# Seven products in another order, a convolution moved to VectorE, and embedding products placed around the last group of a two-block transformer kernel

## What is computed

```python
def conv_glu(h, w_gate, w_up, conv_w, conv_b, w_down):   # block 1, width 2816
    a = h @ w_gate
    u = h @ w_up
    c = conv_b
    for j in range(3):
        c = c + ap[:, j:j + S] * conv_w[j]        # ap: a padded by one token on each side
    return (gelu(c) * u) @ w_down
...
x = x + conv_glu(rmsnorm(x, norm_ffn_g), ...)
gate = sigmoid(rmsnorm(x, norm_ple_g) @ w_ple_gate)
x = x + (p @ w_ple) * gate                         # p: 256 wide, "the embedding"
...
f = square(relu(rms_norm(h, norm2_g) @ w_ff1))     # block 2, width 4096
h = h + f @ w_ff2
gate = sigmoid(rms_norm(h, norm3_g) @ w_ple_gate_2)
h = h + gate * (p_2 @ w_ple_proj_2)
```

## Time and profile before

| | |
|---|---|
| median of 3 runs (3089.62 to 3100.17) | 3090.14 us |
| the profiled execution, its time | 3095.22 us |
| its span in the profile | 3093.4 us |
| TensorE busy | 2879.4 us (93%) |
| VectorE, GpSimd, ScalarE busy | 1841.7, 1183.8, 1010.8 us |
| mean granted clock of TensorE | 0.972 of full speed |

### The profile page before, as it was taken

One profiled execution on the slowest core, in us unless ns is written; L12 is line 12 of the kernel. 1 busy time (PEld: TensorE's weight loads), 2 busy tenths in 40 slices (PEclk: granted clock), 3 DMA queues, 4 the chain that ended last, 5 costly groups with the idle time before them and its releaser, 6 DMA issues. The chain is left out here.

```text
span 3093.4 us, 36229 instructions
## 1 busy us (share of the span) xinstructions
PE 2879.4 (93%) x14210; PEld 2339.4 (76%) x14210; DVE 1841.7 (60%) x2219; ACT 1010.8 (33%) x1476; POOL 1183.8 (38%) x730
## 2 busy tenths in 40 slices
PE   8999999999689898898969999999989999999879
PEld 6888888877577677777748866678868888888767
DVE  8666577776555555555575766663855555555545
ACT  5555433232322222222233344441232222222331
POOL 3111111125555554445534411123555554555332
PEclk9999999999899999999989999999999999999989
DMA  3111001021011111111111200011211111111102
GB/s 119 31 32 30 27 28 35 28 72 38 32 47 45 45 47 45 42 45 44 48 48 66 79 22 21 21 34 35 102 34 52 51 53 55 48 55 52 62 28 81
DMA packets 60767, 145.12 MB, mean 47 GB/s; under 512 B 7616, under 2 KB 8384, under 8 KB 60352
## 3 DMA queue, kind: packets, MB, share of 16 engines
q1 hardware_dynamic: 56288, 128.83, 13.0%
q10 hardware_dynamic: 4320, 14.09, 1.2%
HBM read 132.05 MB, written 8.49 MB: 45 GB/s over the span
## 5 line engine op out<-in xcount | busy, mean ns | idle before, releaser
L892 PE MATMUL ps<-a_hi,w_hi 128*128 128x512 f32 x1184 | 493.2, 417 | 11.6 <-POOL w_lo L766 10.6
L894 PE MATMUL ps<-a_hi,w_lo 128*128 128x512 f32 x1184 | 467.9, 395 | 0.0
L893 PE MATMUL ps<-a_lo,w_hi 128*128 128x512 f32 x1184 | 467.0, 394 | 0.0
L1949 DVE TENSOR_TENSOR x<-ps,x 128x512 f32<-128x512 f32 x432 | 296.8, 690 | 284.4 <-PE ps L1030 283.5
L813 POOL TENSOR_TENSOR w_lo<-w_raw,w_hi 128x512 fp32r<-128x512 f32 x206 | 281.5, 1371 | 395.0 <-ACT w_hi L2279 394.2
L761 POOL TENSOR_TENSOR w_hi<-w_raw,der 128x1024 fp32r<-128x1024 f32 (+1 forms) x61 | 112.7, 1847 | 735.7 <-PE ps L894 568.1
L766 POOL TENSOR_TENSOR w_lo<-w_raw,w_hi 128x1024 fp32r<-128x1024 f32 (+1 forms) x78 | 204.0, 2615 | 286.3 <-ACT w_hi L2279 217.5
L2279 ACT ACTIVATE w_hi<-w_raw 128x512 fp32r<-128x512 f32 (+1 forms) x223 | 145.6, 661 | 453.7 <-PE ps L1030 275.7
L892 PEld LDWEIGHTS ps<-a_hi,w_hi 128*128 128x128 f32 x1184 | 226.3, 191 | 51.6 <-issue 12.4
L894 PEld LDWEIGHTS ps<-a_hi,w_lo 128*128 128x128 f32 x1184 | 225.4, 190 | 49.8
L893 PEld LDWEIGHTS ps<-a_lo,w_hi 128*128 128x128 f32 x1184 | 226.7, 191 | 37.9 <-issue 0.2
(11 more groups left out here) (385 smaller groups left out, 6322.7 us busy)
## 6 DMA issues: line engine op xcount, KB each, us to landing
w_raw<-in_w_mix SPq DMA_DIRECT2D x54, 512.0 KB, 3.5
w_raw<-in_w_f SPq DMA_DIRECT2D x96, 256.0 KB, 2.6
w_raw<-in_w_gu SPq DMA_DIRECT2D x88, 256.0 KB, 2.6
w_raw<-in_w_ple SPq DMA_DIRECT2D x20, 512.0 KB, 3.5
chunk<-in_w_f SPq DMA_DIRECT2D x32, 256.0 KB, 3.1
chunk<-in_w_dn SPq DMA_DIRECT2D x22, 256.0 KB, 3.1
w_raw<-in_w_dn SPq DMA_DIRECT2D x22, 256.0 KB, 3.0
x<-in_x SPq DMA_DIRECT2D x8, 512.0 KB, 7.8
```

The costliest lines, as they stand in the source:

```text
L892: mm(ps[:, bank, :], wh, hi[:, k, cols], start=(k == 0), stop=False)
L893: mm(ps[:, bank, :], wh, lo[:, k, cols], start=False, stop=False)
L894: last = mm(ps[:, bank, :], wl, hi[:, k, cols], start=False, stop=(k == nk - 1))
L1949: tt(x[:, u, c], ps[:, 5 + (2 * KT * (ff.group0 + g) + n) % 3, :], x[:, u, c], ALU.add).then_inc(x_add, 1)
```

## The change

The same products are computed with the same number of matmuls. What moves:

1. **Order of the seven products**: A22, S1, S3, A11, S2, A12, S4, and the down product of the last group goes ahead of number 5 instead of 3. A12 is now added in the bank of A11 after ScalarE has copied A11 out. In block 1 the up tile takes the first column half and the gate tile the second, so that the gate is complete after five products instead of six.
2. **After the products** (VectorE, `lower_row`): five sums in a row after S2; the 16 `add_down` of a group are spread among the pair's own operations (`some`).
3. **Convolution of block 1**: its first tap was a ScalarE operation between VectorE's; now all three taps are on VectorE. The product with `rstd` of the up half is done on the halves of `uv` instead of on the gelu's output.
4. **ScalarE's order**: `gelu` and the high part of the hidden tile of pair q are issued inside pair q+1 (ahead of the entries of S3's and A11's places), not at the end of pair q.
5. **Embedding products**: the first half of the 16 outputs goes between the last pair and the last down product, the second half behind the down product; their weights come through the ring slots.
6. **End of the feed-forward**: the running sum of squares moves from VectorE to GpSimd, the splitting of p too; the weight units' high parts move from GpSimd to ScalarE.
7. **Start**: the high parts of the output units' weights move from GpSimd to ScalarE; the first pair's first four products are interleaved in all four k-steps; in block 2 the last two output units are interleaved by k, so that the operands of x pair 2 are made before they end.
8. **Loads**: quarters 3 and 2 of the next pair are loaded first, then 0 and 1.

```diff
-E_A11, E_S1, E_S2, E_A12, E_S4, E_S3, E_A22 = range(7)
-BANK = (0, 2, 1, 0, 3, 4, 1)
-PRE = 3
+E_A22, E_S1, E_S3, E_A11, E_S2, E_A12, E_S4 = range(7)
+BANK = (0, 1, 2, 3, 4, 3, 4)
+PRE = 5
+DUE = ((E_S3, E_A11), (E_A22, E_S1))
...
 # SyncE: loads
+                for q in range(ff.n_pairs):
+                    if ff.begins(q):
+                        load_chunk(ff, second, g - 1, 0)
+                    if q + 1 < ff.n_pairs:
+                        load_quarter(ff, first, q + 1, 3)
+                        load_quarter(ff, first, q + 1, 2)
+                    else:
+                        load_emb(ff, emb_name, 0, 1)
+                        load_emb(ff, emb_name, 0, 0)
+                    if ff.begins(q):
+                        for c in range(1, 4):
+                            load_chunk(ff, second, g - 1, c)
+                    if q + 1 < ff.n_pairs:
+                        load_quarter(ff, first, q + 1, 0)
+                        load_quarter(ff, first, q + 1, 1)
...
 # GpSimd: end of a feed-forward
+                low(ff.emb_entry(0, 0), quarter[2])
+                low(ff.emb_entry(0, 1), quarter[3])
+                for k in range(PT):
+                    pool.wait_ge(p_hi, 2 * ff.turn + k + 1)
+                    tt(e_lo_[:, k, :], p_raw[:, k, :], e_hi[:, k, :].bitcast(F32), ALU.subtract).then_inc(p_lo, 1)
+                chunk_lows(ff.groups - 1)
+                for k in range(KT):
+                    if k in (0, 2):
+                        low(ff.emb_entry(1, k // 2), quarter[2 + k // 2])
+                    if k == 6:
+                        unit_low(u0)
+                    sums_of_squares(q1, k)
+                unit_low(u0 + 1)
...
 # TensorE: waits of a product, and the end
+                if i == 5:
                     pe.wait_ge(p1_out, n + 1)
                 elif i == 6:
                     pe.wait_ge(f_read, 7 * n + 1)
+                elif q:
+                    pe.wait_ge(f_read, 7 * (n - 1) + (3, 5, 5, 6, 7)[i])
...
+                embed(ff, 0)
+                downward(ff, of, ff.groups - 1)
+                embed(ff, 1)
...
 # VectorE
+            def lower_row(ff, q, first, second, between=(lambda n: None)):
+                tt(uv[:, 0, :], ps[:, bk[E_S2], :], uv[:, 0, :], ALU.add).then_inc(f_read, 1)
+                tt(second, ps[:, bk[E_S3], :], uv[:, 0, :], ALU.add).then_inc(f_read, 1)
+                between(1)
+                tt(first, ps[:, bk[E_A22], :], second, ALU.add).then_inc(f_read, 1)
+                between(1)
+                tt(second, second, ps[:, bk[E_S1], :], ALU.subtract).then_inc(f_read, 1)
+                tt(uv[:, 1, :], uv[:, 0, :], ps[:, bk[E_S1], :], ALU.subtract).then_inc(f_read, 1)
+                between(2)
...
 # ScalarE
             def gelu(q):
-                av(conv[:, :], pad[:, 0:T], ACT.Identity, scale=col("conv_w0", q),
-                   bias=col("conv_b", q)).then_inc(conv_first, 1)
-                act.wait_ge(conv_done, 2 * q + 2)
+                act.wait_ge(conv_done, q + 1)
                 av(conv[:, :], conv[:, :], ACT.Gelu).then_inc(act_done, 1)
...
+            def feed_forward(ff, first_part, second_part, n_stat):
+                for q in range(ff.n_pairs):
+                    for i in range(7):
+                        if i == PRE and ff.begins(q):
+                            for c in range(4):
+                                entry_high(ff, ff.down_entry(q // ff.pairs - 1, c) + 4)
+                        if q and i == ff.first_due:
+                            first_part(q - 1)
+                        if q and i == ff.second_due:
+                            second_part(q - 1)
+                        if i == (E_S2 if q else E_S1):
+                            copy_first(ff, q)
+                        if q + 1 == ff.n_pairs and i == E_S4:
+                            round_embedding(ff.turn)
+                        entry_high(ff, ff.entry(q, i) + 4)
```

More of the change, by code:

```diff
@@ L12 @@
+import itertools
 from contextlib import ExitStack
@@ L838, in feed_forward @@
                     low(ff.entry(q, E_S2), asum[:, :])
-                    if q % ff.pairs == 0 and g:
-                        for c in range(4):
-                            low(ff.down_entry(g - 1, c), quarter[0] if c % 2 else chunk[:, :])
+                    if ff.begins(q):
+                        chunk_lows(q // ff.pairs - 1)
                     low(ff.entry(q, E_A12), quarter[1])
@@ L1063, in feed_forward @@
-                downward(ff, of, slots, ff.groups - 1)
+                        if i == PRE and ff.begins(q):
+                            downward(ff, of, q // ff.pairs - 1)
+                        product(ff, of, q, i)
+                embed(ff, 0)
+                downward(ff, of, ff.groups - 1)
+                embed(ff, 1)
             for k in range(KT + 2):
@@ L2041, in gated_tile @@
+                    dve.wait_ge(rstd_ready, 2)
+                step(tt(gate, gate, rstd[:, :], ALU.mult))
+                some(2)
+                step(ts(conv[:, :], pad[:, 0:T], col("conv_w0", q), col("conv_b", q), ALU.mult, ALU.add))
+                some(2)
+                step(stt(conv[:, :], gate, col("conv_w1", q), conv[:, :], ALU.mult, ALU.add))
+                some(2)
                 stt(conv[:, :], pad[:, 2:T + 2], col("conv_w2", q), conv[:, :], ALU.mult,
                     ALU.add).then_inc(conv_done, 1)
-                lower_left(FF1, q)
+                some(2 * KT)
@@ new lines, in squared_tiles @@
+                    dve.wait_ge(rstd_ready, 5)
+                stt(pad[:, 0:T], pad[:, 0:T], 0.0, rstd[:, :], ALU.max, ALU.mult).then_inc(hid_ready, 1)
+                some(2 * KT)
+                dve.wait_ge(f_full, FF2.done(q, E_A12))
+                stt(uv[:, 0, :], ps[:, bk[E_A12], :], 0.0, rstd[:, 0:HALF], ALU.max, ALU.mult).then_inc(f_read, 1)
+                dve.wait_ge(f_full, FF2.done(q, E_S4))
+                tt(uv[:, 1, :], ps[:, bk[E_S4], :], uv[:, 1, :], ALU.add).then_inc(f_read, 1)
```

760 lines of the change are left out of this document (363 added, 397 removed).

## The result

The changed kernel takes 2922.01 us (median of 4 runs, 2920.46 to 2923.17) against 3089.88 (4 runs, 3088.87 to 3100.17): ratio 0.9449, 95% interval 0.9429 to 0.947. The profiled execution took 2922.56 us. The prediction was 2899 with a range of 2865 to 2945: the direction and the range held, and the gain was 18 us smaller than the sum (172.6 us of span, not 191). The rest of the 23 us between 2899 and 2922 comes from the executions: the profiled one of the kernel before stood 5.3 us above its median, that of the changed kernel 0.6.

What follows compares the result with a forecast made beforehand. TensorE bound it, busy 2879.4 of 3093.4 us. Gains of 111 + 0 + 28 + 27 + 16 + 9 = 191 from 3095.2 gave 2904, less 5.1 for the median 2899 us, range 2865 to 2945.

Steps and rivals of the forecast that it cites:

- the sum: Whole kernel: the gains of all stages added, 111 + 0 + 28 + 27 + 16 + 9 = 191 us.
- Steady part of block 1, 111: Block 1's feed-forward between start and end: the excess of 115.8 us goes, except 5, so 111 us less.
- The walk: Block 1's pair timed operation by operation from its first matmul: hidden tile at 30.7, wanted at 32.7, slack 2.0 us.
- the worst case: Block 1's pair: four VectorE operations each wait out a 1.3 us GpSimd operation; convolution ends 27.1, hidden tile 32.7.
- The 5 us for pauses in first pairs: Steady part of block 1: 5 us of the excess kept for pauses in the first pairs of a group.
- Rival B: Steady parts: VectorE and GpSimd get in each other's way, costing 35 us plus 15 at lower clock; 2949; chance 0.12.
- Steady part of block 2, 0: Block 2's feed-forward between start and end: it has no excess, so the gain is 0.
- Ends, 28 and 27: Ends of the two feed-forwards: each shortened to 53.9 us, 28 us less in block 1 and 27 in block 2.
- the full price: TensorE: 0.2269 us per matmul with nothing in its way, at the full 2.4 GHz clock, read from block 2's feed-forward.
- Rival C: Ends of both feed-forwards keep their length, sums on GpSimd delaying the norm: each 75 us instead of 54; 2941; chance 0.08.
- Start of block 2, 9: Start of block 2's feed-forward: operands of pair 2 made earlier, until about 2280, plus 16.5; 9 us less, bounds 4 and 14.
- Start of block 1, 16: Start of block 1's feed-forward: VectorE's last operand at 798.5, pair 1 at 815 instead of 831.5; 16 us less.

Runs made afterwards that it cites:

- experiment 11: Against the changed kernel, VectorE instead of GpSimd adds the eight squares into ss in the last down product of both blocks: 2916.7 us.
- experiment 10: Against the changed kernel, GpSimd adds the square of tile 6 after the low parts of S3 and A11, in both feed-forwards' first pair: 2913.8 us.

## Why the prediction was right, and where it was off

- **Steady part of block 1, 111: right (116.2), on thinner ice than I wrote.** The walk hit the end of the five sums (17.1 us walked, 17.2 measured) and the start of gelu (25.1, 25.3). The convolution did not end at 21.9 but at 25.3, since all four operations were stretched (7.90 us for 4.73), though not to the 27.1 of the worst case. Gelu was done at 26.4 (walked 26.2), but VectorE reached the product with it only at 28.3, behind the two reads and a product by `rstd` (1.75 us) that the walk had left out. The hidden tile came at 32.9 (walked 30.7, worst 32.7): past the start of the down product at 32.6. That costs nothing only because the down product reads the pair's other tile first, 0.68 us of matmuls that the walk had left out. That this came out at 0.42 us and not below nothing is luck. With the tap doubled, a delay beyond the margin does appear as waits. The 5 us for pauses in first pairs were not needed.
- **Rival B's mechanism is real, its size was wrong.** VectorE and GpSimd do stretch each other: 2.20 us instead of 1.28 for a tap, and 2.0 instead of 1.3 for a low part beside it (the fence below: GpSimd's timeline, two low parts). A full wait for a 1.3 us operation each time would have added 5.2 us; 3.2 were added. The Trainium skill, "SBUF — State Buffer", section "Who interferes with whom", has the second of the two fully blocked. In the 8.0 us of this trace from 955.8 lie VectorE's four operations, 4.6 us by the shortest durations of their lines, and 5.3 us of GpSimd's by its shortest (1.27 for a low part, 1.73 for the sum): mostly one after the other, as the rule has it, with 1.9 us of overlap that it has not. One of the four, the first tap, reads only one operand from SBUF, so this does not test the rule cleanly.

```profile
956.54 3.97 POOL L852 TENSOR_TENSOR w_lo<-w_raw,w_hi 128x512 fp32r<-128x512 f32 x2
```

- **Steady part of block 2, 0: right** (612.0 for 612.6).
- **Ends, 28 and 27: 21.5 and 22.9; the term that was missing is the lower clock.** The sum had 6.5 us of pauses (3 for p's split, 2 for additions, 1.5 for GpSimd's queue) and every matmul at the full price. Of pauses the windows show 8.3 and 6.0, so this part was close in total, though p's split took 5.6 and 3.2 and the additions 0.2 each. But the matmuls took 4.6 and 4.9 us more than their price. Behind the longer pauses they run at the lower level, here behind the waits for p and for the embedding's banks (columns as in the windows; granted clock 0.54, 0.43 us from matmul to matmul):

```profile
1440.27:1447.65 7.38, 5.59 (x13) 3.93 (x14) 3.67 (x4) 0.63 (x2) 6.09 (x3) 0.54 0.13 38
1485.02:1488.60 3.58, 3.58 (x10) 2.82 (x9) 3.58 (x2) 1.12 (x3) 3.58 (x2) 0.54 0.30 58
```

  The rows of the kernel before had it to see: 55.7 to 57.0 us busy for 47.4 at the price. In block 1 I also missed what ScalarE's roundings of p queue behind, an entry that waits 3.9 us for a chunk whose load is issued after p's. And the 1.5 us at GpSimd's queue became 2.5 at the embedding's banks: the same sums, reached through ScalarE. Rival C was right in kind, but experiment 11 gives it 2 to 5 us, not 42.
- **Start of block 2, 9: only 1.3; here the walk failed.** It started from VectorE's last operand and took TensorE to be waiting for it, with 48 large matmuls to go, 16.5 us. The operand came 15.9 us into the window (walked 14), and from there it took 22.6: TensorE still had 63 large matmuls to go. It had waited 8.3 us for the low part of S3, behind a sum of squares that waits for ScalarE's square, which waits for the last unit; and it waited 2.3 us for `sm` later on. The step left GpSimd's order unread. With one instruction moved (experiment 10) 48 are left behind the operand, and 2.7 to 4.7 us come back.
- **Start of block 1, 16: 12.4**, with the operand nearly as predicted (798.5, measured 799.8: 1.3 us of the 3.6 missing). The rest has the same cause: 60 large matmuls stood behind the operand, not 48, after three waits for GpSimd's low parts (11.4 us), and the broadcast waits another 0.9 us for VectorE's `sm`; the 1.8 us for the lower clock were not needed (1.00 there). In experiment 10 it is 48 again, and 16.2 us from the operand to pair 1, where the walk had 16.5.
- **The sum.** The misses are -3.6, +5.2, -6.5, -2.7, -7.7, +0.6 and -4.1, together -18.8, of 191. They do not cancel: every stage that missed by over 1 us fell short, except the one whose allowance of 5 was not needed, and the range held because it had 46 us of room on that side.

**What stays open.** The steady part's 116 us are not split among the edits. Undoing one thing costs 42 (the tap at gelu's place, through A12's bank) or 33.5 (late loads, through the copy of A11). Both waits push TensorE back and so give the other operands time, so they can't be added. The old order of the seven products with the new rest was not tried, so that the order itself gives the remainder is argued only. Likewise the place of the embedding explains 6 to 7 of the 44 us of the ends and the move of the sums of squares none (it cost 2 to 5); that the rest comes from the lows moved off the additions' path, from the units' high parts on ScalarE and from the banks of the embedding was not taken apart.

## What to carry to other kernels

Read a steady part by its slack, not by its waits: TensorE 100% busy can mean 0.42 us or 6 us of room. List every operand's margin, not only the smallest: here they were 0.42, 1.04 and 1.35 us, and the doubled tap, the tap at gelu's place and the late loads all ran into one of the larger two. The same late loads cost 33.5 us in one block and nothing in the other. When an order is rewritten, walk every in-order queue at the places where the program leaves its loop, GpSimd's and the loads' too; the late operands of this prediction stood there, behind an instruction that waits for something unrelated. And where pauses remain, price the matmuls behind them too: at the ends that was more than the error in the pauses. Which engine does an operation mattered less than behind which wait it is issued.

## What was not expected of the hardware

- Short pauses of TensorE cost more than themselves. In the steady part 4.1 us of idle time came with 4.0 us of slower matmuls (tap doubled), 22.0 with 11.5 (late loads), 27.6 with 14.4 (tap at gelu's place), 75.9 with 41.7 (five taps): an idle microsecond cost 1.5 to 2. There are two parts in it. Each pause, even one of 0.36 us with the clock at 1.00, costs about 0.4 us beside its idle time, in the last matmul before it and the first ones behind it (tap doubled: 0.74 us from start to start across the pause, then 0.31, then 0.23). And some pauses are followed by a spell of 7 to 11 matmuls at the lower level, 0.43 us each: none of the eleven with the tap doubled (0.36 to 0.45 us), 5 of the ten with late loads (1.8 to 2.4), 7 of the ten with the tap at gelu's place (nine of 2.5, one of 5.2), all twenty with five taps (3.7 to 3.9). With late loads, pauses at the same place of the program, 2.1 to 2.4 us long, differ in it.
- An operation added to VectorE can take its time from the contention of those behind it: twenty-one doubled taps of 1.39 us on average raised VectorE's busy time by 10.3 us, 0.5 each, and four times as many more by 81.4, 0.97 each.
